# Delta heads: the 2x2 base of the inverse from the gram and per-token weights

## What is computed

```python
decay = exp(where(lower, gc[..., :, None] - gc[..., None, :], -inf))      # gc: cumulative log decay
a = where(strict, einsum('bhncd,bhnsd->bhncs', k * beta, k) * decay, 0.0)
t_inv = triangular_solve(eye + a, eye, lower=True, unit_diagonal=True)
u, w = t_inv @ (v * beta), t_inv @ (k * beta * exp(gc))
# then, chunk by chunk, with the state s:
v_new = u - w @ s
o = (q * exp(gc)) @ s + qk @ v_new
s = s * g_last + k_dec.T @ v_new
```

## Time and profile before

| | us |
|---|---|
| median of 3 runs | 1983.09 |
| lowest, highest | 1980.28, 1990.69 |
| profiled execution | 1983.51 |
| its span, first to last instruction | 1981.7 |
| TensorE matmul busy | 1851.6 (93%) |
| VectorE busy | 1035.7 (52%) |
| ScalarE busy | 618.5 (31%) |
| GpSimd busy | 81.7 (4%) |

### The profile page before, as it was taken

How to read it: one execution, slowest core, us unless ns; L and a number is a source line. 1 busy time by engine, 2 the same in 40 slices (tenths; PEclk the granted TensorE clock), 3 DMA queues, 4 the chain that set the end, 5 groups by cost and what they waited for, 6 DMA issues and landing times. The chain is left out here.

```text
span 1981.7 us, 39070 instructions
## 1 busy us (share of the span) xinstructions
PE 1851.6 (93%) x16132; PEld 1338.0 (68%) x16132; DVE 1035.7 (52%) x2060; ACT 618.5 (31%) x1337; POOL 81.7 (4%) x59
## 2 busy tenths in 40 slices
PE   6999999999999999998888799989989899999997
PEld 2466666666666666544766688767776687888886
DVE  3567575867676776211145567774555792320101
ACT  2334444544444453202023233233332440100000
POOL 1000000101010110000000000010000000000000
PEclk8999999999999999998999899989999899999999
DMA  9121313121111012031311433231102223443434
GB/s 347 74 98 43 108 45 112 49 66 44 34 34 39 29 43 77 7 142 53 133 43 43 163 128 114 78 107 59 51 34 80 86 102 110 166 158 139 170 149 149
DMA packets 52237, 183.63 MB, mean 93 GB/s; under 512 B 5856, under 2 KB 9312, under 8 KB 51808
## 3 DMA queue, kind: packets, MB, share of 16 engines
q1 hardware_dynamic: 52064, 181.18, 25.3%
HBM read 179.06 MB, written 2.10 MB: 91 GB/s over the span
## 5 line engine op out<-in xcount | busy, mean ns | idle before, releaser
L857 PE MATMUL banks<-u,w_ring 128*128 128x512 f32 x768 | 367.1, 604 | 2.0 <-DVE u L690 2.0
L379 PE MATMUL banks<-u,w_ring 128*128 128x256 f32 x1056 | 251.2, 390 | 8.4 <-PEq L188 8.4
L379 PEld LDWEIGHTS banks<-u,w_ring 128*128 128x128 f32 x1056 | 199.7, 195 | 42.2 <-issue 17.1
L857 PEld LDWEIGHTS banks<-u,w_ring 128*128 128x128 f32 x768 | 137.9, 192 | 111.5 <-issue 102.9
L403 PE MATMUL banks<-u,w_ring 128*128 128x256 f32 x640 | 138.4, 379 | 0.5 <-PEq L188 0.5
L403 PEld LDWEIGHTS banks<-u,w_ring 128*128 128x128 f32 x640 | 121.5, 190 | 17.3 <-issue 0.8
L889 DVE SCALAR_TENSOR_TENSOR acc<-raw,hc,acc 128x512 f32<-128x512 f32 x128 | 107.8, 842 | 4.6
L3439 PE MATMUL banks<-gated,w_ring 128*128 128x512 f32 (+1 forms) x288 | 96.8, 498 | 1.8 <-PEq L188 1.8
L3439 PEld LDWEIGHTS banks<-gated,w_ring 128*128 128x128 f32 x288 | 54.6, 190 | 44.1 <-issue 40.8
L3439 PE MATMUL banks<-ffn,w_ring 128*128 128x256 f32 x352 | 79.2, 389 | 3.0 <-PEq L188 3.0
L3439 PEld LDWEIGHTS banks<-ffn,w_ring 128*128 128x128 f32 x352 | 68.8, 196 | 13.3 <-issue 3.3
(11 more groups left out here) (525 smaller groups left out, 3110.8 us busy)
## 6 DMA issues: line engine op xcount, KB each, us to landing
w_ring<-in_w SPq DMA_DIRECT2D x289, 512.0 KB, 5.6
gated<-in_ada SPq DMA_DIRECT2D x32, 512.0 KB, 4.8
h<-in_h SPq DMA_DIRECT2D x2, 2048.0 KB, 10.8
hold<-h SPq DMA_DIRECT2D x1, 1024.0 KB, 5.2
h<-hold SPq DMA_DIRECT2D x1, 1024.0 KB, 9.6
out<-u SPq DMA_DIRECT2D x8, 128.0 KB, 1.9
const_base<-in_const SPq DMA_DIRECT2D x1, 896.0 KB, 11.3
const_part<-in_const SPq DMA_DIRECT2D x1, 640.0 KB, 4.3
```

The source lines that it names most:

```text
L379: mm = self.nc.tensor.matmul(place, self.st.chunk(g % 2, slot)[:, P * k:P * k + P], self.src(k), start=(k == 0), stop=(k == KT - 1))
L857: mm = nc.tensor.matmul(self.places[m % len(self.places)][:, :], (st.slot(m) if g is None else st.chunk(g % 2, m))[:, P * k:P * k + P], u[ ...
```

## The change

The base of the inverse is no longer cut out of the turned `a_t`. `cells` (GpSimd) masks the gram with the 2x2 pattern, four instructions of 64 partitions by 256 elements. `swap` (TensorE) exchanges the betas of neighbouring tokens with four small matmuls. `weights` (VectorE) multiplies them by the new column `EA`. `base` (VectorE) multiplies masked gram and weights and subtracts from the identity, two instructions of 128x512 per direction. It stands before the head that uses it, between the `chain` calls. The sixteen transposes and their waits are gone, and the keys and values are turned behind silu 4, both. One product moves from the transition to the pause before L1290 (`REST`), and in heads 4 to 6 one moves from behind L1230 to behind L1213. A stage may now have 66 semaphores in place of 60.

```diff
-QUANT = 6                         # columns kept per head
+QUANT = 7                         # one more: EA, the exponential of a token's log decay
 # opening, ScalarE, behind g_ready
+            link(nc.scalar.activation(ea, lg, ACT.Exp), s["e_ready"])
 # opening, VectorE: for each direction also
+                link(put(EA, ea, d))
 # Front.mean: k_inv made in place; the scaling of the columns now signals "normed"
+            def swap(self, pe):
+                pe.wait_ge(self.s["normed"], self.up("normed", 1))
+                for d in range(2):
+                    for hb in range(2):
+                        beta = self.hs[half(hb), 4 * TT * BETA:4 * TT * BETA + 4 * TT].rearrange("p (j d t) -> p d j t", j=2, d=2)[:, d]
+                        mm = nc.tensor.matmul(bank[2][half(hb), 16 + 8 * d:24 + 8 * d], C(f"lev_{'bf'[d]}0")[half(hb), half(hb)], beta,
+                                              start=True, stop=True)
+                mm.then_inc(self.s["swapped"], 1)
+            def cells(self, pool):
+                pool.wait_ge(self.s["kq_done"], self.up("kq_done", 1))
+                for d in range(2):
+                    for hb in range(2):
+                        done = nc.gpsimd.tensor_tensor(pair_gram[half(hb), d], four(gram)[half(hb), :, half(hb)],
+                                                       C(f"lev_{'fb'[d]}0")[half(hb), 0:64].unsqueeze(1).to_broadcast([64, TT, 64]), ALU.mult)
+                done.then_inc(self.s["cells"], 1)
+            def weights(self, dve, link):
+                dve.wait_ge(self.s["swapped"], self.up("swapped", 1))
+                grown = self.hs[:, 4 * TT * EA:4 * TT * EA + 4 * TT].rearrange("p (j d t) -> p d t j", j=2, d=2)
+                link(nc.vector.tensor_tensor(pair_w, bank[2][:, 16:32].rearrange("p (d j t) -> p d t j", d=2, j=2), grown,
+                                             ALU.mult))
+            def base(self, dve, link, d):
+                dve.wait_ge(self.s["cells"], self.up("cells", 1))
+                mine = inv[:, d].rearrange("p (t j) e -> p t j e", j=2)
+                link(nc.vector.tensor_tensor(mine, pair_gram[:, d].unsqueeze(2).to_broadcast([P, TT, 2, 64]),
+                                             pair_w[:, d].unsqueeze(3).to_broadcast([P, TT, 2, 64]), ALU.mult))
+                link(nc.vector.tensor_tensor(inv[:, d], eye[:, :].unsqueeze(1).to_broadcast([P, 2 * TT, 64]), inv[:, d], ALU.subtract),
+                     self.s["based"])
 # pool_head, behind the output's norm
+                if more:
+                    front.cells(pool)
 # tensor_head, the transition
-                for c in (0, 2, 1, 3):
-                    if made:
-                        pe.wait_ge(s["chained"], made.up("chained", c + 1))
...
-                    for t in range(TT):
-                        mm = nc.tensor.transpose(tile(bank[2 * (c % 2) + c // 2], t), tile(a_t[:, c, :], t), C("ident"))
-                    mm.then_inc(s["a_done"], 1)
 # tensor_head: border(1, d) and turn(0, d) wait for "based"; border(1, d) also for "chained" 3 + d
 # tensor_head, filler
-REST = (2, 2, 3)
+REST = (2, 2, 4)
-                ahead(LAST)                       # behind the off-diagonal sums
+                ahead(LAST if n < 4 else 2 * LAST)
-                ahead(2 * LAST)                   # behind the low blocks
+                ahead(2 * LAST if n < 4 else LAST)
 # tensor_head, behind the output's turns, before rows 2 and 3
+                    front.swap(pe)
 # vector_head, start
-                for d in range(2):
...
-                    dve.wait_ge(s["a_done"], due("a_done", 2 * d + 2))
-                    for hb in range(2):
-                        blocks_a = banks[half(hb), 2 * d:2 * d + 2, :].rearrange("p j (t e) -> p j t e", e=P)[:, :, :, half(hb)]
-                        link(nc.vector.tensor_tensor(by_chain(inv[half(hb), d]), blocks_a, mask(d, 0)[half(hb)], ALU.mult))
-                    mine = inv[:, d]
-                    link(nc.vector.tensor_tensor(mine, eye[:, :].unsqueeze(1).to_broadcast([P, 2 * TT, 64]), mine, ALU.subtract), s["t_ready"])
# vector_head, end, with the next head's front
                     front.chain(dve, link, 1)
                     output(1)
+                    front.silu(dve, link, 3)
+                    front.weights(dve, link)
+                    front.base(dve, link, 0)
                     front.chain(dve, link, 2)
+                    front.base(dve, link, 1)
                     front.chain(dve, link, 3)
-                    front.silu(dve, link, 3)
```

More of the change, by code:

```diff
@@ L736, in _ @@
             front.silu(dve, link, 3)
-            for c in range(4):
-                front.chain(dve, link, c)
+            front.chain(dve, link, 0)
+            front.chain(dve, link, 1)
+            front.weights(dve, link)
+            front.base(dve, link, 0)
+            front.base(dve, link, 1)
+            front.chain(dve, link, 2)
+            front.chain(dve, link, 3)
     for sem in (h_loaded, first_loaded, ab_loaded, masks_loaded):
@@ L828, in delta_heads @@
                   "o_sum": 1, "o_sqd": 1, "o_mean": 1, "o_root": 1, "o_norm": 1, "o_turned": 2, "o_out": 2,
-                  "proj": 6, "raw_out": 4, "conv": 4, "tanh": 4, "silu": 4, "squared": 2, "ssum": 1, "mean": 1, "root": 1, "grams": 2, "kq_done": 2, "scal": 1, "rows": 4, "dec_ready": 4, "chained": 4, "gate_in": 2}
+                  "proj": 6, "raw_out": 4, "conv": 4, "tanh": 4, "silu": 4, "squared": 2, "ssum": 1, "mean": 1, "root": 1, "grams": 2, "kq_done": 2, "scal": 1, "rows": 4, "dec_ready": 4, "chained": 4, "gate_in": 2,
+                  "normed": 1, "swapped": 1, "cells": 1, "based": 2}
         class Front:
@@ L995, in load_rest @@
             sp.dma_start(held[:, p, :], ada[4 * r + p]).then_inc(m_sems[p], 16)
-        front_names = ("proj raw_out conv tanh silu squared ssum mean root grams kq_done scal rows dec_ready chained "
+        front_names = ("proj raw_out conv tanh silu squared ssum mean root grams kq_done scal rows dec_ready chained normed swapped cells based "
                        "gate_in")
@@ L1118, in tensor_head, with inverse_ready @@
                 mm.then_inc(s["turned"], 1)
+                if made:
+                    pe.wait_ge(s["dec_ready"], made.up("dec_ready", 4))
+                    pe.wait_ge(s["o_out"], 2 * n)
+                def inverse_ready(lv, d):
+                    if lv:
+                        pe.wait_ge(s["t_ready"], due("t_ready", 2 * (lv - 1) + d + 1))
+                    elif made:
+                        pe.wait_ge(s["based"], made.up("based", d + 1))
                 quarters = [(t, j, hb) for t in range(TT) for j in range(2) for hb in range(2)]
                 def border(lv, d):
-                    pe.wait_ge(s["t_ready"], due("t_ready", 2 * (lv - 1) + d + 1))
+                    inverse_ready(lv - 1, d)
+                    if lv == 1 and made:
+                        pe.wait_ge(s["chained"], made.up("chained", 3 + d))
                     for t, j, hb in quarters:
@@ L1130, in turn @@
                 def turn(lv, d):
[L1132 removed]
+                    inverse_ready(lv, d)
                     if lv:
@@ L1202, in tensor_head @@
                 last = LEVELS - 2
-                pe.wait_ge(s["t_ready"], due("t_ready", 2 * last + 1))
+                inverse_ready(last, 0)
                 pe.wait_ge(s["t_out"], due("t_out", 2 * last))
@@ L1207, in tensor_head @@
                 ahead(LAST)
-                pe.wait_ge(s["t_ready"], due("t_ready", 2 * last + 2))
+                inverse_ready(last, 1)
                 for t in range(TT):
```

39 lines of the change are left out of this document (22 added, 17 removed).

## The result

The kernel after takes 1996.22 us (median of 11 runs, 1989.71 to 2009.55), the kernel before beside it 1983.69 (11 runs, 1980.28 to 1990.69). The ratio is 1.006, 95% interval 1.0044 to 1.0077: the change makes the kernel 12.5 us slower. The profiled execution after took 2001.6 us (span 1999.9), one of the longer ones, so I read places and durations from it and take the size from the medians.

The account below looks back on a forecast made before the run. VectorE's unbroken list, not TensorE, was taken to bound the transition. 1983.5 - 1.9 (opening) + 4.2 (seven transitions) + 3.6 (clock) = 1989.4 us, 1989 on the median's footing; range 1972 to 1996.

Parts of the forecast that it names:

- Rival 1: Levels 1 and 2 of heads 1 to 7: clock falls in every transition, 8.4 to 11.9 us, 1995; chance 0.18.
- the main case: Whole kernel: opening, seven transitions and three clock falls give 1989, own range 1984 to 1995; chance 0.48.
- VectorE, not TensorE, ends the transition: Transition: VectorE's list is unbroken and ends last, so the transposes' 2.1 us a head on TensorE are worth 0.
- Rival 3: Transition: TensorE is the bound after all, 2.1 + 0.7 us saved in eight heads, 1961; chance 0.09.
- The hold: Transition: four GpSimd cells instructions each hold VectorE 0.45 us, +1.8 us a head, bounds 0 to 3.2.
- Rival 2: Transition: GpSimd doesn't hold VectorE, so 1973, or 1974 with one fall of the clock; chance 0.25.
- The transition's sum: VectorE per transition: -1.19 + 1.8 = +0.6 us; seven give +4.2, between -8.3 and +14.
- VectorE's -1.19: Transition, base on VectorE alone: -2.88 for four L1404, +1.44 for two multiplications, +0.25 for weights, per head.
- The wait for the first update: TensorE before update (1,0): waits near 2 us for L1411; idle from 197 to 203 grows to some 3.5 us.
- Swap and filler: Transition on TensorE: four small matmuls a head and the moved products stay hidden beside VectorE, 0 us.
- Opening and head 0: Start of the delta part: two column copies +0.5, earlier first update -2.4, together -1.9 us, bounds -3.5 and 0.
- The clock: First levels behind transitions: half clock costs 1.2 us each, three of seven hit, +3.6, bounds 0 and +11.9.

Follow-up runs that it names:

- e7: Changed kernel plus sixteen unread transposes of the keys' tile on TensorE just before border (1,0): 1984.10 us, ratio 0.9991.
- e2: Changed kernel with GpSimd's four masked gram copies replaced by one memset, so the inverse's base is the identity: 1983.36 us, ratio 0.9993.
- e4: Kernel before plus only the four masked gram copies on GpSimd, waited for but not read: 1995.66 us, ratio 1.005.
- e8: Kernel before with only the change's two filler edits (REST, and one product moved in heads 4 to 6): 1986.28 us, ratio 1.0003.
- e1: Changed kernel plus two unread 128x512 matmuls before the first update of heads 1 to 7: 1984.61 us, ratio 0.9993.
- e10: Changed kernel plus one unread 128x512 matmul before the first update of heads 1 to 7: 1987.41 us, ratio 1.0013.
- e11: Kernel before with the output's norm multiplication (L1049) moved from GpSimd to VectorE, inside the convolution: 1982.25 us, ratio 0.9985.
- e5: Changed kernel without GpSimd's cells: ScalarE copies gram blocks, VectorE masks them, values' turns precede the first update: 1986.98 us, ratio 1.001.
- e6: e5 plus one idle 128x512 matmul ahead of the values' turns, before the first update: 1983.95 us, ratio 0.9998.

## Why the prediction came out as it did

The prediction has the parts of the mechanism and not its size: 1989 was said, 1996.22 measured, at the range's upper end of 1996. Of these 7.2 us, 0.6 are the kernel before, which is 1983.69 beside it and was 1983.09 then; the change was put at +5.9 and is +12.5. By the prediction's own line of 1993 the kernel is slower, which had a chance of 0.28. Rival 1, the clock in every transition (1995, chance 0.18), is what happened. The range's upper end was set by that rival and not by the main case (1984 to 1995), so a result near that end speaks for the rival.

- **VectorE, not TensorE, ends the transition.** Right: e7 put sixteen transposes back and T stayed at 17.23. Rival 3 is out.
- **The hold.** Right in kind, 1.48 us where 1.8 was said (T in e2 against after; 1.49 in e4), 0.37 for each of the four instructions. They hold less than I took, though they last longer: 717 ns at least against my 0.55, the four 3.75 us while VectorE competes. L1099, as L1049 before it, holds for 1.65 of its 1.90. So both hold for their record less about 0.3 us. The Trainium skill (SBUF — State Buffer, "SBUF: two separate sides"), by which the whole instruction is locked, would give 2.9 us, an estimate by the 0.72 us record; e2 and e4 measured half of that. Rival 2 is out.
- **The transition's sum.** +0.25 measured, +0.6 said. The difference is the hold (0.3); VectorE's -1.19 came as -1.23 (0.25 less 1.48).
- **The wait for the first update.** 2.11 us, near 2 said, and 0.50 at border (1, 1): together 2.6 us of idle time, where some 3.5 was worked out.
- **Swap and filler at nothing.** Right: eight records, 0.40 us together, beside VectorE's list; e8's ratio is 1.0003 (0.9989 to 1.0017), its T 16.98.
- **Opening and head 0.** -1.9 said, -1.0 at the first update. The stage's first work starts later (102.33 in place of 100.72), but that start moves by as much between profiles of kernels with the same opening. The first update came at 106.5 to 109.1 us in four profiles with the new opening and base (after, e1, e7, e10; mean 107.5) and at 108.0 to 110.5 in four with the old ones (before, e4, e8, e11; mean 109.6). So the sign is shown and -1.9 may be right; the two profiles compared here can't tell. From TensorE's first work to the first update it is 4.65 us in place of 7.3, near the 4.5 said:

```profile
102.33 0.63 PE L1156 MATMUL banks<-const_base,y 128*128 128x128 f32 x4 [2.53 <-PEq L218]
...
106.98 0.65 PE L1206 MATMUL banks<-dec,acc 64*64 64x64 f32 x32
```

- **The clock: the step that failed.** I wrote "How many of seven transitions are hit depends on phase, 0 to 7. I take three: +3.6". It was seven of seven, two of them twice as long. The price was well taken: 1.2 said, 1.15 to 1.6 measured. Seven at about 1.3 (the mean of those three), and two second halves at the same price, make 11.7 where I had 3.6: 8.1 us too little. The better sum of the seven transitions takes 2.5 off that and head 0 adds 0.9, which makes 6.5 of the 6.6 by which +12.5 exceeds +5.9. That it comes out so closely is luck: the price is the mean of three heads, and in heads 0 to 2 and 7 the pauses of the earlier trace rows's kind hide it. The ground given for three was phase, and against rival 1 that the levels start anew at 202. The traces show otherwise: the stop comes at the same place in every head, and each time a fall begins between 0.8 us before and 1.6 us behind the first update. No row stood behind my three. In the earlier trace rows the clock fell behind 1.2 us of pause among small matmuls, and I had worked out 3.5 us of idle time; the same trace also held the pause of 1.71 us at 762.1, shown above, with no fall behind it. From the two, all or none of seven like standstills could be argued, and three could not.

Two things stay open. By T and by the falls at the transitions, e5 and e6 should be some 3.5 us faster than before, and they measured the same; the pauses once per 256 instructions may carry the difference, but nothing I ran changes them alone. And what makes the clock fall behind 2.6 us of idle time in every head, and behind other pauses of 1.2 to 2.6 us only sometimes, isn't shown; no run has a length between 1.6 and 2.6 us in the transition.

## What to carry to other kernels

Before you take work off an engine that waits for another, work out how long it will then stand, and look in the trace for what the clock did behind pauses of that length among small matmuls. If it fell behind one of them, remember that the new standstill comes at the same place with the same length every time: let the case in which it falls at every repetition have its full price and a real chance, and don't settle on a share in between. A few matmuls that nobody reads, put in front of the wait, tell in one run whether the clock is the cost. And an elementwise instruction moved to GpSimd isn't free when VectorE reads two tensors in SBUF beside it: here a 1024-element one cost VectorE 1.65 us to save it 1.23.

## What the runs showed of the hardware

- GpSimd's power of 128x8 (L141, 1.87 us) holds nothing: the L904 beside it keep their 0.75 us, while L1099 of the same length costs them 1.65. A long instruction with little data and a long one with much are different neighbours.
- GpSimd's cost isn't proportional: 64x256 takes at least 0.72 us and 128x1024 1.90, which makes, by an estimate from the two, 1.5 ns an element of the free dimension and 0.3 us fixed. That fixed part is about what both lack of a full hold.
- 3.4 us at 1.2 GHz cost about 1.3 us in the levels, where TensorE and VectorE wait for each other in turn, and 6.8 us cost 2.7. A standstill of 2.11 us, 2.1 us behind one of 0.50, brought a fall in seven of seven transitions. One of 0.94 us (e7), 1.21 us (e2), 1.34 us (e5) or of 0.50 and 1.06 (e10) did so in none of the seven of its profile, and e2's one fall, at 213.9, came with a pause of 1.51 us that waits for no engine, 15 us behind the first update.
- TensorE's pauses with no releaser come 193 or 194 of its records behind a multiple of 256, in all 14 profiles (36 pauses of 0.4 to 2.6 us). All 36 lie among the small matmuls of the levels, and not every such place has one in every run.
